# Query and sub-key products: one fp32 product, or three fp32r products of high and low parts

## The reference, cut to what matters

```
def peer(h, wq, subkeys, u_tab, v_tab):       # h: 512 tokens x 1024
    q = (ht @ wq).reshape(T, PEER_HEADS, 2, PEER_HALF)          # 512 x 8 x 2 x 128
    sc = jnp.einsum('thpd,hpnd->thpn', q, subkeys, preferred_element_type=jnp.float32)
    v1, i1 = lax.top_k(sc[:, :, 0], PEER_TOPK)                  # 16 best of 128
    v2, i2 = lax.top_k(sc[:, :, 1], PEER_TOPK)
    cand = (v1[..., :, None] + v2[..., None, :]).reshape(...)
    best, pos = lax.top_k(cand, PEER_TOPK)
    ...
```

## Time and profile before

| | |
|---|---|
| median of 3 runs | 2850.21 (2845.07 to 2852.61) |
| the profiled execution, its own time | 2846.21 |
| its span, first to last instruction | 2844.4 |
| mean granted PE clock | 0.996 of 2.4 GHz |
| PE busy | 2798.4 (98%) |
| PEld, DVE, ACT, POOL busy | 2400.5, 1764.0, 971.8, 1595.6 |
| all of L860 (the scores), start of first to start of last | 186.3 to 271.8 |

### The profile page before, as it was taken

How to read it: one execution, slowest core, us unless ns; L and a number is a source line. 1 busy time by engine, 2 the same in 40 slices (tenths; PEclk the granted TensorE clock), 3 DMA queues, 4 the chain that set the end, 5 groups by cost and what they waited for, 6 DMA issues and landing times.

```text
span 2844.4 us, 39077 instructions
## 1 busy us (share of the span) xinstructions
PE 2798.4 (98%) x14439; PEld 2400.5 (84%) x14439; DVE 1764.0 (62%) x2551; ACT 971.8 (34%) x1388; POOL 1595.6 (56%) x1653
## 2 busy tenths in 40 slices
PE   8899999999999999999999999999999999999999
PEld 6798888888888899999998796588888878988887
DVE  6568999997662378888887956854333353433333
ACT  4532333322222333333334547743121232331121
POOL 5444878787777368777741431025555536455553
PEclk9999999999999999999999999999999999999999
DMA  6942445488885689999993321012222222222221
GB/s 202 340 149 83 141 143 157 143 314 326 317 313 157 215 301 353 366 353 367 367 362 126 108 70 46 1 55 99 97 96 96 90 82 98 87 97 96 97 101 68
DMA packets 195766, 503.39 MB, mean 177 GB/s; under 512 B 31672, under 2 KB 83000, under 8 KB 195000
## 3 DMA queue, kind: packets, MB, share of 16 engines
q1 hardware_dynamic: 108624, 343.09, 35.3%
q10 hardware_dynamic: 52200, 91.23, 9.1%
q0 software_dynamic: 34816, 67.41, 6.7%
HBM read 432.76 MB, written 64.68 MB: 175 GB/s over the span
## 4 chain that ended last, share of the span: by engine, by line
PE 95%; DVE 3%; ACT 1%; DMA 1%; issue 0%; SPq 0%; ACTq 0%; DVEq 0%
PE ps L662 29%; PE ps L664 29%; PE ps L663 29%; PE ps L1019 2%; PE ps L1039 1%; PE ps L1030 1%; PE ps L950 1%; PE ps L860 1%; DMA unit_raw<-w_units 0%; DVE std L1651 0%; DVE swa_small L1813 0%; DVE swa_e L1808 0%; PE ps L882 0%; PE ps L1060 0%; ACT Ed L1533 0%
## 5 line engine op out<-in xcount | busy, mean ns | idle before, releaser
L558 POOL TENSOR_TENSOR unit_lo<-unit_raw,unit_hi 128x256 fp32r<-128x256 f32 x984 | 761.1, 809 | 765.3 <-ACT unit_hi L1183 764.6
L662 PE MATMUL ps<-hn_hi,unit_hi 128*128 128x512 f32 (+1 forms) x2352 | 909.9, 387 | 18.8 <-DVE hn_lo L1752 11.6
L664 PE MATMUL ps<-hn_hi,unit_lo 128*128 128x512 f32 (+1 forms) x2352 | 895.7, 381 | 0.0
L663 PE MATMUL ps<-hn_lo,unit_hi 128*128 128x512 f32 (+1 forms) x2352 | 895.5, 381 | 0.0
L1183 ACT ACTIVATE unit_hi<-unit_raw 128x1024 fp32r<-128x1024 f32 x486 | 506.0, 1055 | 457.2 <-DMA unit_raw<-w_units 357.4
L662 PEld LDWEIGHTS ps<-hn_hi,unit_hi 128*128 128x128 f32 x2352 | 442.7, 188 | 118.7 <-POOL unit_lo L558 9.4
L590 POOL DMA_INDIRECT gate_dram<-gate_sums,gate_at x384 | 463.4, 1207 | 133.3 <-issue 123.1
L663 PEld LDWEIGHTS ps<-hn_lo,unit_hi 128*128 128x128 f32 x2352 | 442.9, 188 | 86.8 <-issue 4.5
L664 PEld LDWEIGHTS ps<-hn_hi,unit_lo 128*128 128x128 f32 x2352 | 442.5, 188 | 85.4
L662 PE MATMUL ps<-gp_hi,unit_hi 128*128 128x384 f32 x1024 | 343.9, 336 | 4.0 <-DVE gp_lo L2052 4.0
L663 PE MATMUL ps<-gp_lo,unit_hi 128*128 128x384 f32 x1024 | 343.1, 335 | 0.0
(11 more groups left out here) (285 smaller groups left out, 3932.8 us busy)
## 6 DMA issues: line engine op xcount, KB each, us to landing
unit_raw<-w_units SPq DMA_DIRECT2D x486, 512.0 KB, 3.9
araw<-ada_units SPq DMA_DIRECT2D x96, 512.0 KB, 6.0
act_dram<-stage ACTq DMA_DIRECT2D x32, 1024.0 KB, 6.7
gate_dram<-zero SPq DMA_DIRECT2D x8, 3072.0 KB, 23.9
abuf<-act_dram ACTq DMA_DIRECT2D x32, 768.0 KB, 7.6
gbuf<-gate_dram ACTq DMA_DIRECT2D x15, 1536.0 KB, 20.5
gate_dram<-gate_sums,gate_at POOLq DMA_INDIRECT x384
x<-x_t SPq DMA_DIRECT2D x8, 256.0 KB, 6.1
```

The lines of the kernel that those rows point to most:

```text
L558: last = nc.gpsimd.tensor_tensor(lo[:, u % RING, cols], raw[:, u % RING, cols], hi[:, u % RING, cols].bitcast(F32), ALU.subtract)
L662: mm(dst, wh, ah, start=start, stop=False)
L663: mm(dst, wh, al, start=False, stop=False)
L664: return mm(dst, wl, ah, start=False, stop=stop)
```

## The change

Queries and sub-keys are each split in a high part (rounded to fp32r) and a low part (the rest), and each fp32 product becomes three fp32r products: high by high, high by low, low by high. For this
- ACT writes its copy of the query as fp32r (`qh_hi`), and makes the sub-keys' high parts in four pieces of 128 x 512 (`subkeys_high`): one ahead of the loop, one behind each of the first three copies;
- DVE gets 16 subtractions of 128 x 512 from PSUM (`query_low`) and 4 of SBUF alone (`subkeys_low`), placed ahead of the search of the half before;
- PE waits for `q_low` in place of `q_ev`, and at every fourth half for `subk_low`;
- three new semaphores take the place of five: the 9 batches of picks share 4 semaphores with summed counts. That moves no instruction.

```diff
+        subk_lo = at("subk_lo", R2, [P, 2 * PEER_HEADS, P], F32R)
+        subk_hi = at("subk_hi", R2 + 14 * KB, [P, 2 * PEER_HEADS, P], F32R)
+        qh_hi = at("qh_hi", R2 + 8 * KB, [P, 2, T], F32R)
+        qh_lo = at("qh_lo", R2 + 22 * KB, [P, 2, T], F32R)
...
             def scores(n):
-                pe.wait_ge(q_ev, n + 1)
+                pe.wait_ge(q_low, n + 1)
+                if n % 4 == 0:
+                    pe.wait_ge(subk_low, n // 4 + 1)
                 if n >= 4:
                     pe.wait_ge(tk_done, n - 3)
                 for t in range(TT):
-                    last = mm(ps[:, 4 + n % 4, t * P:(t + 1) * P], qh[:, n % 2, t * P:(t + 1) * P], subk[:, n, :],
-                              start=True, stop=True)
+                    tok = slice(t * P, (t + 1) * P)
+                    dst, q_hi = ps[:, 4 + n % 4, tok], qh_hi[:, n % 2, tok]
+                    mm(dst, q_hi, subk_hi[:, n, :], start=True, stop=False)
+                    mm(dst, q_hi, subk_lo[:, n, :], start=False, stop=False)
+                    last = mm(dst, qh_lo[:, n % 2, tok], subk_hi[:, n, :], start=False, stop=True)
                 last.then_inc(sc_ready, 1)
...
+            def subkeys_high(k):
+                four = slice(4 * k, 4 * k + 4)
+                activation(subk_hi[:, four], subk[:, four], ACT.Copy).then_inc(subk_high, 1)
+            act.wait_ge(subk_in, 16)
+            subkeys_high(0)
             for n in range(2 * PEER_HEADS):
                 used(U_WQ + n)
                 if n >= 2:
                     act.wait_ge(sc_ready, n - 1)
-                activation(qh[:, n % 2], ps[:, n % 4, :], ACT.Copy).then_inc(q_ev, 1)
+                activation(qh_hi[:, n % 2], ps[:, n % 4, :], ACT.Copy).then_inc(q_ev, 1)
+                if n < 3:
+                    subkeys_high(n + 1)
                 split_hi(U_WQ + n + AHEAD)
...
+            def subkeys_low(k):
+                four = slice(4 * k, 4 * k + 4)
+                dve.wait_ge(subk_high, k + 1)
+                V.tensor_tensor(subk_lo[:, four], subk[:, four], subk_hi[:, four].bitcast(F32), ALU.subtract)\
+                    .then_inc(subk_low, 1)
+            def query_low(n):
+                dve.wait_ge(q_ev, n + 1)
+                V.tensor_tensor(qh_lo[:, n % 2], ps[:, n % 4, :], qh_hi[:, n % 2].bitcast(F32), ALU.subtract)\
+                    .then_inc(q_low, 1)
+            subkeys_low(0)
+            query_low(0)
             for n in range(2 * PEER_HEADS):
+                if n + 1 < 2 * PEER_HEADS:
+                    query_low(n + 1)
+                if n < 3:
+                    subkeys_low(n + 1)
                 dve.wait_ge(sc_ready, n + 1)
```

More of the change, by code:

```diff
@@ L93 @@
 PICK_OF = [b for b, n in enumerate(PICKS) for _ in range(n)]
+PICK_SEMS = 4
 LAG = AHEAD - 1
@@ L198, in build_program @@
         subk = at("subk", R2, [P, 2 * PEER_HEADS, P])
-        qh = at("qh", R2 + 8 * KB, [P, 2, T])
+        subk_lo = at("subk_lo", R2, [P, 2 * PEER_HEADS, P], F32R)
+        subk_hi = at("subk_hi", R2 + 14 * KB, [P, 2 * PEER_HEADS, P], F32R)
+        qh_hi = at("qh_hi", R2 + 8 * KB, [P, 2, T], F32R)
+        qh_lo = at("qh_lo", R2 + 22 * KB, [P, 2, T], F32R)
         left = at("left", R2 + 12 * KB, [P, TT, P])
@@ L345, in build_program @@
         scattered = [sem(f"scattered{t}") for t in range(TT - 1)]
-        picks_in = [sem(f"picks_in{b}") for b in range(len(PICKS))]
+        picks_in = [sem(f"picks_in{b}") for b in range(PICK_SEMS)]
         rows_in = [sem(f"rows_in{k}") for k in range(ROWS)]
@@ L380, in build_program @@
         q_ev = sem("q_ev")
+        q_low = sem("q_low")
+        subk_high, subk_low = sem("subk_high"), sem("subk_low")
         tk_done = sem("tk_done")
@@ L577, in pick @@
                                         bass.IndirectOffsetOnAxis(act_at[:, k:k + 1], 0))\
-                    .then_inc(picks_in[PICK_OF[k]], 16)
+                    .then_inc(picks_in[PICK_OF[k] % PICK_SEMS], 16)
             def fetch(k):
@@ L2064, in weigh_picks @@
                 cols = slice(PICK_AT[b], PICK_AT[b + 1])
-                dve.wait_ge(picks_in[b], 16 * PICKS[b])
+                dve.wait_ge(picks_in[b % PICK_SEMS], 16 * sum(PICKS[b % PICK_SEMS:b + 1:PICK_SEMS]))
                 link(V.tensor_tensor(picked[:, cols], picked[:, cols], mine[:, cols], ALU.mult))
```

## The result

The changed kernel took 2858.42 us (median of 20 runs, 2851.76 to 2877.49), the kernel before, run beside it, 2852.37 (20 runs, 2845.07 to 2859.49). The ratio of the two sets of runs is 1.0026 with a 95% interval of 1.0016 to 1.0037: +7.4 us, 4.6 to 10.6. It isn't the quotient of the two medians, which lie 6.1 us apart. The forecast was 2857.8, from +7.6 us on the 2850.21 known then. The move is clear of zero, and its middle lies under the 8.5 us that were named as the bound of "the same".

What follows compares the result with a forecast made beforehand. PE was taken to bound the kernel, its stream's changes going whole into the end. +7.1 us on PE, +0.3 for DVE at the start and +0.2 at the last `scores` make +7.6 on 2850.21: 2857.8 us, range 2849 to 2864.

Steps and rivals of the forecast that it cites:

- What bounds: Query stage, 183 to 272 us: PE busy in all 89.00 us, so each us its stream grows goes whole into the end.
- The price of a narrow fp32r product: In `scores`: each fp32r product with 128 moving columns is bound by its stationary operand's load, 0.111 us.
- The sum on PE: Twelve products for eight passes: one `scores` takes 1.33 us instead of 0.89, +0.44; sixteen of them +7.1 us.
- DVE at the start: First halves of the query stage: slow SBUF subtractions make PE wait some 0.1 us at three halves, +0.3 us.
- The last `scores`: At `scores(15)`: copy, then subtraction and signals, 1.44 us plus 0.06, against 1.33 of cover, +0.2 us.
- The cover behind the stage: Key units: DVE's lag does not grow, tightest low parts have 4.6 us of slack, so nothing absorbs the 7.6.
- The load at 0.120: Rival for `scores`: an fp32r load costs 0.120 us, +8.8 and 0.1 at the end, 2859.1 us; chance 0.20.
- Streaming: Rival for `scores`: streaming binds at 0.067 us, DVE then bounds the start; +0.5 to +1.8, 2850.7 to 2852.0; chance 0.13.
- Narrow fp32r as dear as fp32: Rival for `scores`: a product under 256 columns costs 0.222 us, +28 us in 16, 2878.5 us; chance 0.15.
- Slow DVE: Rival: searches and subtractions stretch beside POOL's work, the new coupling costs over 3 us more, 2861 to 2866; chance 0.05.
- Same or slower: Whole time: 8.5 us (about 0.3%) bounds no change; chances faster 0.01, same 0.50, slower 0.49.

Runs made afterwards that it cites:

- PE's part alone: Changed kernel without low parts or DVE subtractions: all three fp32r products high by high, PE waiting for ACT's high parts; 2858.95 us, ratio 1.0011 to the kernel before.

## Why the prediction was right, point by point

- **What bounds.** Right. PE was full in the stage but for the wait of 0.3, and in the 148 us behind it, and what the stage lost is whole after the key units (707.6 in both). At the end of the kernel it arrived 0.6 to 3 us short for the changed kernel; whether that is scatter is open.
- **The price of a narrow fp32r product.** Forecast 0.111, by the nearest rows, against bounds of 0.067 and 0.120. Measured 0.112 in the stream, and shown by the halved stationary operand (0.059) and the shortened moving one (0.111 on average) to be the load. By the Trainium skill, "TensorE: Matmul & The Clock Gate", section "LDWEIGHTS (loading the stationary operand)", a load takes P/1.2 ns, 107 ns for 128 columns. The measured 112 ns lie 5 above it. Section "Back-to-back issue gap" of that page of the Trainium skill gives 81 ns for a stream with loads at 128 columns. No stream of 128 x 128 products here ran at that.
- **The sum on PE.** Forecast +7.1, measured +7.65 with PE's part alone. The term was a little small: the step grew by 0.49, not 0.44. By the timeline 0.46 of it lie between the first product of `scores` and the second wide one (1.58 against 1.12). The rest is that the next eight distances of 512-column products are 0.232 on average, where they were 0.228 in the kernel before. Why, no run shows.
- **DVE at the start.** Forecast 0.3, measured nothing: the four subtractions of sub-keys took 0.68 to 0.76, near the low end of the range, and the slack for `scores(2)` was 0.58 where 0.4 was worked out.
- **The last `scores`.** Forecast +0.2, measured +0.3, by the named chain. So of the three terms one was 0.55 too small, one 0.3 too large and one 0.1 too small: the sum, +7.6 for +7.98, is nearer than its largest term.
- **The cover behind the stage.** No wait of PE appeared among the key units, as forecast: they took 707.6 before and after.
- **The rivals.** The load at 0.120: out. Streaming: out as what binds here. Its price was too high as well, 0.059 instead of 0.067, for I had carried over the 0.0135 that wide products have on top of their columns. What it said of DVE is right: with half the stationary columns the products went on at 0.059, and the stage still took 85.7, +0.2, where that rival has +0.5; with one product DVE was late by 3.38 us at the end. Narrow fp32r as dear as fp32: out. Slow DVE: out.
- **Same or slower.** That it would lie near the bound of what can be told was right, and 20 runs told it from zero. By the whole time alone the forecast (+7.6) can't be told from the load at 0.120 (+8.9); the distances in the trace do that. That 2857.8 came within 0.6 of the measured median is in part luck: it stands on 2850.21, a median of three runs, 2.2 below that of twenty, while the medians differ by 6.1 and not by 7.6.

## What to carry to other kernels

Count loads, not columns, where the moving operand has 128 columns or fewer and the stationary one 128: three fp32r products with a 128-column stationary operand cost 3 x 0.111, an fp32 one 2 x 0.111, so splitting pays only for wide moving operands (three of 512 columns took 0.68, one `scores` in fp32 0.89). Before making PE's part of a pipelined step cheaper, work out the other engines' step and above all the last one, where nothing covers their lag: with a third of the products PE still won nothing.

## What the runs showed of the hardware beyond the forecast

- With 64 stationary columns, fp32r products of 128 moving columns followed each other after 0.059, while products of 256 and 512 columns have 0.0135 on top of their columns (0.120 and 0.2265). What is left over is 0.006 for the narrow ones.
- The first narrow product behind a wide one is followed after 0.06 too (206.33, 206.39), with 128 stationary columns. How it escapes the 0.11 of the load is not shown: its successor's load is recorded to start at 206.34, with the product itself.
- In the one profile with 32 moving columns in two of three products, the two `scores` in a row were followed by a granted clock of 0.57 for 4 us (mostly its lower level, 1.2 GHz), without an idle PE but for 0.17. The full three products at the same place, and 36 in place of 12, kept it at 1.00, and so did the twelve with 64 stationary columns. What brought it down is not shown.
